# First expert layer: tokens sorted by group into five tiles, token tiles stationary and weights moving

## What is computed

```python
g_logits = xf @ w_rg + b_rg                       # 4 groups
g_sel = argmax(g_logits); p_g = softmax(g_logits)[g_sel]
e_logits = (xf @ w_re + b_re)[group g_sel]        # 4 experts of that group
top_p, top_i = top_k(softmax(e_logits), 2)        # two of the four
weights = p_g * top_p / sum(top_p)
for e in range(16):
    h = silu(xt @ w_gate[e]) * (xt @ w_up[e])     # 1024 -> 256
    y = y + combine[:, e:e+1] * (h @ w_down[e])   # 256 -> 1024
```

## Time and profile before

| | us |
|---|---|
| median of three runs | 2250.8 |
| lowest and highest run | 2247.23, 2251.64 |
| profiled execution, its span | 2245.4 |
| TensorE busy in it | 2185.8 |
| DVE, ACT, GpSimd busy in it | 1368.7, 764.9, 517.5 |

### The profile page before, as it was taken

One profiled execution on the slowest core, in us unless ns is written; L12 is line 12 of the kernel. 1 busy time (PEld: TensorE's weight loads), 2 busy tenths in 40 slices (PEclk: granted clock), 3 DMA queues, 4 the chain that ended last, 5 costly groups with the idle time before them and its releaser, 6 DMA issues.

```text
span 2245.4 us, 31895 instructions
## 1 busy us (share of the span) xinstructions
PE 2185.8 (97%) x13297; PEld 1905.4 (85%) x13297; DVE 1368.7 (61%) x1770; ACT 764.9 (34%) x1075; POOL 517.5 (23%) x243
## 2 busy tenths in 40 slices
PE   7989999999999999999999999999999999899998
PEld 7889999988888888757988888898888888679998
DVE  6567875577775247796677772246655226765443
ACT  4344444432222232374322222242222223454443
POOL 0014542122221100153122221112222110243431
PEclk9999999999999999999999999999999999999999
DMA  5347876656664336301366653346663336205664
GB/s 163 106 103 213 220 224 182 176 169 175 177 173 115 92 104 180 95 20 57 110 175 185 183 155 91 97 113 187 187 187 110 96 97 168 80 1 144 179 170 147
DMA packets 474005, 314.68 MB, mean 140 GB/s; under 512 B 27503, under 2 KB 435958, under 8 KB 473862
## 3 DMA queue, kind: packets, MB, share of 16 engines
q1 hardware_dynamic: 434304, 237.02, 37.8%
q10 hardware_dynamic: 39558, 75.64, 10.8%
HBM read 311.56 MB, written 1.05 MB: 139 GB/s over the span
## 4 chain that ended last, share of the span: by engine, by line
PE 85%; DVE 8%; ACT 3%; DMA 2%; issue 1%; SPq 1%; POOL 0%; DVEq 0%; ACTq 0%
PE ps L1864 26%; PE ps L1866 25%; PE ps L1865 25%; DVE w_lo L1046 3%; PE ps L2048 2%; ACT w_hi L601 2%; PE ps L1857 2%; PE ps L2491 1%; PE ps L2453 1%; DVE st L1703 1%; DMA raw<-in_w_ffn_down 1%; DVE u_lo L1139 1%; DMA raw<-in_w_in 1%; SPq L572 1%; DVE tmp_a L1131 1%
## 5 line engine op out<-in xcount | busy, mean ns | idle before, releaser
L1864 PE MATMUL ps<-u_hi,w_hi 128*128 128x256 f32 (+2 forms) x2624 | 887.3, 338 | 16.5 <-DVE u_lo L1139 6.2
L1866 PE MATMUL ps<-u_hi,w_lo 128*128 128x256 f32 (+2 forms) x2624 | 875.6, 334 | 0.0
L1865 PE MATMUL ps<-u_lo,w_hi 128*128 128x256 f32 (+2 forms) x2624 | 875.2, 334 | 0.0
L1046 DVE TENSOR_TENSOR w_lo<-raw,w_hi 128x2048 fp32r<-128x2048 f32 (+1 forms) x238 | 504.4, 2119 | 341.2 <-ACT w_hi L601 340.9
L601 ACT CAST w_hi<-raw 128x2048 fp32r<-128x2048 f32 (+1 forms) x238 | 418.4, 1758 | 468.7 <-PE ps L1866 411.9
L1864 PEld LDWEIGHTS ps<-u_hi,w_hi 128*128 128x128 f32 x2624 | 500.4, 191 | 69.8 <-DVE w_lo L1046 9.7
L1866 PEld LDWEIGHTS ps<-u_hi,w_lo 128*128 128x128 f32 x2624 | 500.2, 191 | 49.0
L1865 PEld LDWEIGHTS ps<-u_lo,w_hi 128*128 128x128 f32 x2624 | 500.7, 191 | 46.9
L1785 POOL TENSOR_TENSOR hf_lo<-tmp_b,hf_hi 128x512 fp32r<-128x512 f32 (+1 forms) x88 | 240.6, 2734 | 713.2 <-ACT hf_hi L744 713.2
L1067 DVE SCALAR_TENSOR_TENSOR ada_acc<-ada_w,sc_c,ada_acc 128x512 f32<-128x512 f32 x448 | 348.3, 834 | 7.8 <-DMA ada_w<-in_w_ada 2.0
L1864 PE MATMUL ps<-hf_hi,w_hi 128*128 128x512 f32 (+1 forms) x770 | 270.6, 351 | 1.0 <-DVE w_lo L1046 0.8
(11 more groups left out here) (314 smaller groups left out, 1903.9 us busy)
## 6 DMA issues: line engine op xcount, KB each, us to landing
ada_w<-in_w_ada ACTq DMA_DIRECT2D x144, 512.0 KB, 4.0
raw<-in_w_ffn_gate SPq DMA_DIRECT2D x88, 512.0 KB, 4.0
raw<-in_w_ffn_up SPq DMA_DIRECT2D x88, 512.0 KB, 5.3
raw<-in_w_in SPq DMA_DIRECT2D x52, 512.0 KB, 5.0
raw<-in_w_ffn_down SPq DMA_DIRECT2D x64, 384.0 KB, 3.6
raw<-in_w_ffn_down SPq DMA_DIRECT2D x64, 320.0 KB, 4.2
raw<-in_w_expert_gate SPq DMA_DIRECT2D x32, 512.0 KB, 4.5
raw<-in_w_expert_up SPq DMA_DIRECT2D x32, 512.0 KB, 5.9
```

The source lines that it names most:

```text
L1046: tt(w_lo[:, slot, 0:elems], raw[:, slot, 0:elems], w_hi[:, slot, 0:elems].bitcast(F32), ALU.subtract).then_inc(lo_done.sem, 1)
L1864: mm(acc, w1, m_hi, start=(first and i == 0), stop=False)
L1865: mm(acc, w1, m_lo, start=False, stop=False)
L1866: ins = mm(acc, w2, m_hi, start=False, stop=(last and i == n - 1))
```

## The change

The tokens are sorted by their group into five tiles of 128 slots: one tile for each group, and a fifth for the tokens of one group that has more than 128. For each tile the four experts of its group are computed, 20 steps in all. For the fifth tile the group is read from a register at run time.

- **Router first.** From the one-hot of the group TensorE computes each token's position in its group; DVE turns it into a slot, and compares it with the slot numbers: `place`, a 0/1 matrix (scaled by 1/1024) of 256 tokens by 640 slots. TensorE turns the tokens (`turn_tokens`), and `place` gathers them: `gather` for four tiles, `gather_spill` for the fifth. The results are the tiles' high and low parts `x_hi`, `x_lo`, `xb_hi`, `xb_lo`. Shares are gathered in the same way (`slot_shares`).
- **A step.** The token tile is stationary, and the weights move, 512 columns at a time: 8 x 3 matmuls give gate and up for 128 slots, side by side in one bank. ACT takes silu, DVE multiplies it with the share and the up part in one instruction (`hid`). TensorE turns the result (`turn_hidden`), ACT and DVE make its two parts, and 12 matmuls of 512 columns give the down product, summed over the tile's four experts in two banks. The down product of step i-1 stands behind the gate and up products of step i.
- **Tiles back to tokens.** A finished tile gets its two parts in place of its tokens, and at the end `scatter` multiplies with the turned `place_t`: 80 matmuls of 256 columns for the 8 rows.
- **Weights.** A step has three units of 1 MB: the upper and the lower half of gate and up, and down. In the stage there are five raw buffers (two more in the region, one in `h2`) and three for the parts (the third in `u_hi`, `u_lo`), each waiting for its own predecessor. Rows of a load are 1024 bytes or more (512 before in gate, up and down).
- **Who does what.** DVE makes all low parts of the weights, of the hidden tile and of the finished tiles; GpSimd does nothing in the loop. The quarters of the modulation lie in steps 1 to 16. The context's sums of squares go to GpSimd's start, its root and reciprocal into the router; the context rows go to steps 18 and 19.
- **Closing.** The sums of squares of the tokens for the final norm are kept in `sq_rows` and summed by GpSimd late; the first unit of `f1a` is written out behind the scatter.

```diff
-        st_moe_a = streamed("moe_a", MOE_F, MOE_F, UNIT)
-        st_moe_b = streamed("moe_b", 16, 8, UNIT)
+        st_moe = streamed("moe", 3 * STEPS, KD, UNIT)
...
+        RAW_RING, W_RING = (2, 3, 4, 0, 1), (0, 1, 2)
+        raw_of = [RAW_RING[(u - M0) % 5] if M0 <= u < M1 else u % 2 for u in range(N_UNITS)]
+        w_of = [W_RING[(u - M0) % 3] if M0 <= u < M1 else u % 2 for u in range(N_UNITS)]
...
+            for i in range(STEPS):
+                if i:
+                    hidden_high(i - 1)
+                    split_hi(gate_unit(i) + 3)
+                for c, quarter in ada_at("moe", i)[0]:
+                    ada_load(0, c, quarter)
+                act.wait_ge(unit_done.sem, gate_unit(i) + 2)
+                nc.scalar.activation(gated_up[:, i % 2, :], ps[:, i % 2, 0:HID], ACT.Silu).then_inc(ev["m_silu"], 1)
...
+                split_hi(gate_unit(i) + (4 if i else 3))
+                if i:
+                    split_hi(gate_unit(i) + 5)
+                else:
+                    split_hi(gate_unit(i) + 4)
+                if i and i % 4 == 0:
+                    tile_high(i // 4 - 1)
...
+            dve.wait_ge(ev["ctx_root"], 1)
+            nc.vector.reciprocal(rstd[:, SEQ:T2], rstd[:, SEQ:T2]).then_inc(ev["ctx_rstd"], 1)
...
+            for t in range(2):
+                ins = ts(place[:, t, 0:4 * P], slot_ids[:, 0:4 * P], slot[:, t:t + 1], None, ALU.is_equal)
+            ins.then_inc(ev["places"], 1)
...
+            for i in range(STEPS):
+                if i:
+                    hidden_low(i - 1)
+                    split_lo(gate_unit(i) + 3)
...
+                dve.wait_ge(ev["m_silu"], i + 1)
+                stt(out=hid[:, i % 2, :], in0=gated_up[:, i % 2, :], scalar=share[:, i // 4, i % 4:i % 4 + 1],
+                    in1=ps[:, i % 2, HID:2 * HID], op0=ALU.mult, op1=ALU.mult).then_inc(ev["m_hid"], 1)
...
+                split_lo(gate_unit(i) + (4 if i else 3))
+                split_lo(gate_unit(i) + (5 if i else 4))
+                if i and i % 4 == 0:
+                    tile_rest(i // 4 - 1)
...
+                for c, quarter in work:
+                    ada_quarter(c, quarter)
+                if i >= STEPS - 2:
+                    context_rows_of(4 * (i - STEPS + 2), 4 * (i - STEPS + 2) + 4)
+            hidden_low(STEPS - 1)
+            tile_rest(TILES - 1)
...
+            def up_part(i, k):
...
+                mm(acc, m_hi, high, start=(k == 0), stop=False)
+                mm(acc, m_lo, high, start=False, stop=False)
+                ins = mm(acc, m_hi, low, start=False, stop=(k == KD - 1))
...
+            def down_part(i):
+
+                u, e = down_unit(i), i % 4
+                begin(u, None)
+                pe.wait_ge(ev["ht_low"], i + 1)
...
+            gather(0)
+            gather(1)
+            begin(M0, None)
+            for k in range(KD):
...
+                up_part(0, k)
+                if k + 2 < KD:
+                    gather(k + 2)
+            slot_shares()
+            for i in range(1, STEPS):
+                begin(gate_unit(i), None)
...
+                for k in range(4):
+                    up_part(i, k)
+                    if k == 1:
+                        turn_hidden(i - 1)
...
+                begin(gate_unit(i) + 1, None)
+                for k in range(4, KD):
+                    up_part(i, k)
...
+                down_part(i - 1)
+            turn_hidden(STEPS - 1)
+            pe.wait_ge(ev["place_rows"], TILES)
+            scatter(0, 0, TILES - 1)
+            scatter(1, 0, TILES - 1)
+            down_part(STEPS - 1)
```

More of the change, by code:

```diff
@@ L846, in _ @@
             plain_high_rows("ffn1", SEQ, st_out1["u0"] + 5)
+            for j in range(8):
+                act.wait_ge(ev["u_turned"], j + 1)
+                ut = ut_lo if j % 2 else ut_hi
+                c0 = 512 * (j // 4)
+                nc.scalar.copy(ut[:, j // 2 % 2, c0:c0 + 512], ps[:, j % 4, :]).then_inc(ev["u_rows"], 1)
+            split_hi(M0 + 2)
             act.wait_ge(ev["g_shift"], 1)
@@ L1581, in modulation @@
+            tt(r4a[:, :, :], r4a[:, :, :], spread(r1a[:, :]), ALU.mult).then_inc(ev["shares"], 1)
+            tile_low(7)
+            split_lo(M0 + 2)
             def modulation(l, nw, m):
@@ new lines, in gather_spill @@
+            def gather_spill(r):
+                pe.wait_ge(ev["spill_places"], 1)
+                for bank, ut in ((6, ut_hi), (7, ut_lo)):
+                    if r:
+                        pe.wait_ge(ev["xb_low" if bank == 7 else "xb_high"], 1)
+                    for k in range(4 * r, 4 * r + 4):
+                        for t in range(2):
+                            c0 = P * (k % 4)
+                            ins = mm(ps[:, bank, c0:c0 + P], ut[:, t, P * k:P * k + P], place[:, t, 4 * P:SLOTS],
+                                     start=(t == 0), stop=(t == 1))
+                    ins.then_inc(ev["spilled"], 1)
@@ new lines, in turn_hidden @@
+            def turn_hidden(i):
+                pe.wait_ge(ev["m_hid"], i + 1)
+                if i:
+                    pe.wait_ge(ev["ht_low"], i)
+                for k in range(2):
+                    c0 = HID * (i % 2) + P * k
+                    ins = turn(ps[:, 5, c0:c0 + P], hid[:, i % 2, P * k:P * k + P], P)
+                ins.then_inc(ev["hid_turned"], 1)
+            def down_part(i):
+                u, e = down_unit(i), i % 4
+                begin(u, None)
+                pe.wait_ge(ev["ht_low"], i + 1)
+                if e == 0 and i:
+                    pe.wait_ge(ev["y_low"], i // 2)
+                if i == 0:
+                    pe.wait_ge(ev["x_low"], KD)
+                for half in range(2):
+                    acc = wide(2 + half)
+                    for k in range(2):
+                        m_hi, m_lo = ht_hi[:, i % 2, k, :], ht_lo[:, i % 2, k, :]
+                        high, low = [two_eighths(u, w, uw, 4 * k + 2 * half) for w, uw in ((w_hi, u_hi), (w_lo, u_lo))]
+                        first, final = e == 0 and k == 0, e == 3 and k == 1
+                        mm(acc, m_hi, high, start=first, stop=False)
+                        mm(acc, m_lo, high, start=False, stop=False)
+                        ins = mm(acc, m_hi, low, start=False, stop=final)
+                ins.then_inc(unit_done.sem, 1)
@@ new lines, in scatter @@
+            def scatter(k, t0, t1):
+                if t1 == TILES:
+                    pe.wait_ge(ev["y_low"], 2 * TILES)
+                for t in range(t0, t1):
+                    for part in range(2):
+                        ins = mm(row_sum(k), tile_out(t, part)[:, k, :], place_t[:, t, :], start=(t == 0 and part == 0),
+                                 stop=(t == TILES - 1 and part == 1))
+                if t1 == TILES:
+                    ins.then_inc(ev["row_sums"], 1)
+            n0, e1 = norm_of["l0a"], norm_of["end1"]
```

661 lines of the change are left out of this document (406 added, 255 removed).

## The result

The changed kernel takes 2254.8 us (median of 20 runs, 2249.3 to 2259.9), the kernel before 2250.7 beside it: a ratio of 1.0018, 95% interval 1.0010 to 1.0027. That is 0.2% slower, where 2217 was forecast. The profiled execution has a span of 2256.4 us, 11.0 more than before. The medians differ by 4.1 only: the profiled execution of before (2247.2) was 3.5 us faster than its median, and that of the changed kernel (2258.3) 3.6 slower. So dates taken from the two profiles make the change look some 7 us worse than the medians do.

What follows compares the result with a forecast made beforehand. DVE was to bound the expert steps at 11.4 us: step 1 at 184.5, steps 1 to 16 end at 366.9, second unit at 423.8 against 457.2. The gain of 33.4 gives 2212.0, plus 5.4, 2217 (forecast 2209 to 2228, range 2200 to 2250).

Steps and rivals of the forecast that it cites:

- DVE becomes the bound: Expert steps 1 to 16: DVE's work of 10.9 us plus stalls makes 11.4 a step, over TensorE's 8.2 plus 0.3.
- The ada quarter: DVE in steps 1 to 16: a quarter of a modulation chunk, 4 instructions of 0.80 us, 3.2 a step.
- the stall ahead of the third low part: DVE in each step: it waits 0.2 us for ACT's cast into the buffer freed by the down product.
- the prediction's own sign of being right: Expert stage: DVE busy over 90%, TensorE's idle time ended by the hidden tile's low part, steps of about 11.4 us.
- rival 2: Expert stage: the clock falls before all 19 down products, 2.4 us each, giving 2258; chance with other slower outcomes 0.12.
- the odds of one in eight: Down products: one in eight was taken to run cold, at 2.4 us more, counted as 0.3 us a step.
- the forecast's gap of 2.6: Expert steps: all TensorE idle time, 11.1 - 8.5 = 2.6 us, gathers ahead of each down product.
- The squares on GpSimd at nothing: Ahead of the causal masks: 15 sums, 14 us, fit GpSimd's idle 75.7 us and were costed at nothing.
- the head's total: Router to step 1: router work, positions, gathers, first products and shares put step 1's start at 184.5 us, kept 180 to 190.
- The tail: From step 17 to the next stage's second unit: from 366.9 us to 423.8, against 457.2 before.
- DMA at 345 GB/s: Expert loads with rows of 1024 bytes or more: 345 GB/s, 10.6 us a step, just under DVE's time.
- rival 1: Expert loads: DMA is the bound at 291 GB/s, 12.6 us a step in sixteen steps, giving 2238; chance 0.18.

Runs made afterwards that it cites:

- sums_behind_down: The changed kernel with the ada sums behind the step's down product and DVE's addition of their result just ahead of its ada quarter: 2227.9 us, ratio 0.9918.
- warm_wait: The changed kernel with 22 unread products of 512 columns put ahead of the ada sums in steps 5, 9, 13 and 17: 2242.9 us, ratio 0.9977.
- late_squares: The changed kernel with the context's squares on GpSimd behind the four causal masks instead of ahead of them: 2248.2 us, ratio 0.9992.
- three_edits: The changed kernel with sums_behind_down, late_squares and the last step's hidden parts ahead of the next stage's work together: 2218.5 us, ratio 0.9871.
- light_quarters: sums_behind_down with most of DVE's modulation work in the stage cut and all loads kept, so the modulation is not the reference's: 2204.1 us, ratio 0.9804.

## Why the prediction was wrong

- **DVE becomes the bound, 11.4 us a step: right for a step without a wait.** Its ordinary step is 10.5, and 11.7 with a finished tile, 10.8 on average. The ada quarter takes 2.73 where 3.2 was counted, the stall ahead of the third low part 0.4 to 0.5 where 0.2 was, and one of sixteen down products was cold where two were counted. Of steps 1 to 16, the 13 that don't stall take 145.2 us for a forecast of 148.2. The first four of them are longer, 11.3, 11.5, 11.1 and 13.2 us; the fourth has the cold product, and the rest was not followed.
- **The step that failed: the modulation was counted as DVE's work and as bytes, and never as a wait of TensorE.** The prediction asked what is queued behind the wait of the down product, and did not ask it of `ada_sums`, although the code puts it into the middle of the product that the silu waits for. Steps 5, 9 and 13 take 54.8 us where 34.2 were forecast, and step 17 takes 16.2 for 8.7: 28 us in the profile, of which moving the sums got back 22.5 in the kernel's time. So the prediction's own sign of being right, DVE busy over 90%, failed at 83%. In the kernel before the same sums cost 1.68 us, since TensorE was the last to be ready there. Moving the bound to DVE turned a free rendezvous into a stall.
- **The clock (rival 2): right in kind, wrong in place.** The gaps ahead of the down products came out at 0.9 to 1.6 us, not 2.6, and the clock held over them: 1.00 in all three steps between two stalls. That kept the rival away, and not the odds of one in eight: in the nine kernels traced with this stage, all 16 gaps of 2.56 to 2.79 us ahead of a down product were followed by six to eight cold products, the 7 of 2.23 to 2.25 us by cold ones twice, and the 56 of 0.88 to 1.66 us never. With the forecast's gap of 2.6 in every step its condition would have held each time, at about 1 us a step (11.5 against 10.5 in sums_behind_down; an estimate) and not 2.4, since only part of the product was cold. That the gap was shorter was luck. The four waits of 5.2 us brought the clock to 0.50, which is 1.2 GHz, for 10.2 to 10.4 us each. Its price there, 14.5 us of DVE's idle time (warm_wait), is a third of the 41 that the rival put on it. The Trainium skill, "TensorE: Matmul & The Clock Gate" (its first part, on the clock gate), says that the low clock is the default and activity lifts it; warm_wait, where useless products made the kernel 9 us faster, agrees.
- **The squares on GpSimd at nothing: wrong, 5.9 us.** The prediction looked only at whether GpSimd had time. What DVE does beside it in these 17 us was not asked; the cost is on DVE, and the router starts 7.2 us late. Less this shift step 1 starts at 184.1 (185.9 in late_squares, 185.2 in three_edits), forecast 184.5. That the head's total is right is luck in part: the first wide product starts at 166.2, less the shift 4 us ahead of the forecast's 163, and from there to step 1 it takes 25.1 us where 21.5 were counted.
- **The tail: 19.6 us worse.** 7.5 are the stall of step 17. In step 18 it is 1.3, and in step 19 it is 6.9: the prediction put DVE at 10.7 us of work there, and missed that ACT's cast of the next stage's second unit waits for a load issued at 423.83, 5.31 us long, with the context rows and the last hidden part queued behind it. The final down product ran cold for the most part, as forecast. From the last hidden part to the second unit it took 30.3 for 26.5. Most of this is the final mean: its last four rows are summed among the products of the next unit, and the first normed row comes at 458.96, 7.0 us behind the last scatter product (450.68 and 1.29), where the old closing's 4.6 was kept. Putting the hidden part first got back about 3 us, with overlapping intervals.
- **DMA at 345 GB/s (rival 1 refuted): right.** 190 to 230 us of the changed kernel ran at 349 GB/s with a share of 1.04, 230 to 270 of light_quarters at 365. The rule of the Trainium skill, "DMA: Bandwidth & Descriptors" (Specifications), line rate from 512 bytes on, does not fit: the earlier trace rows had 291 at 512-byte rows, and rows of 1024 bytes and more give 365. The stages say the same, less strictly: GB/s divided by the share was 210 / 0.76 = 276 before and is 301 / 0.89 = 338 in steps 1 to 16. No run changed the row length alone.

## What to carry to other kernels

When a change makes another engine the bound, go through every semaphore of the old bound once more: each wait that was free because it always came last is now paid, with all that is queued behind it, and the clock can double it. Put a sum of finished work at the end of the in-order queue's step, behind the product that waits for the same engine anyway. A helper on GpSimd is not free where DVE has short work on SBUF; look at which instructions of DVE run beside it, and not only at GpSimd's idle time.

## What the runs showed of the hardware

- The clock fell for 10.2 to 10.4 us at waits of 5.2, and at 2.4 us of waiting with 1.95 to 2.95 us of one-column products after it. Behind gaps of 2.56 to 2.79 us in a busy stage it fell for most of one down product in 16 cases of 16, behind 2.23 to 2.25 us in 2 of 7, behind the one gap of 1.85 us (light_quarters, 269.78) it fell, and it held over all 56 gaps of 0.88 to 1.66 us. It held through 1.84 us of one-column products that followed directly on a product of 512 columns (sums_behind_down, four times); behind 1.95 us of them and a wait of 0.18 (warm_wait) it held three times and fell once.
- At half clock products of 512 columns are 0.43 apart and 16 one-column products take up to 3.57 us; at full clock 0.23 and 1.84.
- DVE's short instructions on SBUF take 0.3 to 0.4 us longer beside GpSimd's sums (0.43 to 0.85, 0.76 to 1.18, 0.44 to 0.85). Its subtractions of 2.3 us take no longer, while GpSimd's instructions take up to 2.65 for 0.61.
- Loads with rows of 1024 bytes and more, from two queues, reach 365 GB/s over 40 us, at a share of 1.08.
